# Sample steps spread over the stages, deeper rings for sample data, and row factors of two norms applied later

## The reference, cut to what matters

```
def decoder_layer(x, mk, mv, s0, buf, pos0, p):
    mix, s_new, buf_new = token_mix(rmsnorm(x, p['norm_mix_g']), s0, buf, pos0, p)
    h = x + mix
    h = h + cross_attn(rmsnorm(h, p['norm_x_g']), mk, mv, p['w_xq'], p['w_xo'])
    h = h + sq_relu_mlp(rmsnorm(h, p['norm_mlp_g']), p['w_up'], p['w_down'])
    return h, s_new, buf_new
# token_mix: proj = xn @ w_in -> q, k, v, gz, og, u, ga, gb
#   log_a = log_sigmoid(gz @ w_gk_up + b_gk) / 16
#   o, s_new = gla(q, k, v, log_a, s0): S_t = diag(a_t) S_{t-1} + k_t^T v_t, o_t = q_t S_t
#   branch_a = (rmsnorm(o, gla_norm_g) * silu(og)) @ w_branch_a
#   branch_b = pool_mix(u) @ w_branch_b       (trailing means of 2, 4, 8, 16 rows)
#   mix = (sigmoid(ga) * branch_a + sigmoid(gb) * branch_b) @ w_out
# cross_attn: softmax(q k^T / 16) v, 4 heads, 256 memory rows;  sq_relu_mlp: relu(x @ w_up)**2 @ w_down
```

## Time and profile before

| | |
|---|---|
| median of three runs | 1592.8 us (1590.46 to 1640.49) |
| profiled execution | 1591.72 us |
| its span on the slowest core | 1590.2 us (other cores from 1567.2) |
| PE, DVE, ACT, POOL busy | 84%, 40%, 29%, 13% of the span |
| mean granted TensorE clock of that core | 0.938 of full speed |
| moved by DMA | 265.59 MB, mean 167 GB/s |

### The profile page before, as it was taken

How to read it: one execution, slowest core, us unless ns; L and a number is a source line. 1 busy time by engine, 2 the same in 40 slices (tenths; PEclk the granted TensorE clock), 3 DMA queues, 4 the chain that set the end, 5 groups by cost and what they waited for, 6 DMA issues and landing times.

```text
span 1590.2 us, 21667 instructions; the slowest of 8 cores (1567.2 to 1590.2 us)
## 1 busy us (share of the span) xinstructions
PE 1343.2 (84%) x7848; PEld 659.4 (41%) x7848; DVE 641.9 (40%) x1105; ACT 462.3 (29%) x931; POOL 206.8 (13%) x284
## 2 busy tenths in 40 slices
PE   0884988999999989974879999999987449999997
PEld 0341533444445434432334544544443225444443
DVE  1352322544545325542355623553425014345334
ACT  2252321531256215300104621531114115152111
POOL 3122010310102002100010200300111112020000
PEclk9997899999999999976889999999998759999998
DMA  9969799859896699789875522525688852420232
GB/s 205 176 126 196 150 216 182 202 110 179 221 227 164 153 211 264 163 232 256 196 233 201 190 80 106 146 93 199 165 188 202 191 141 95 159 107 27 107 121 99
DMA packets 49252, 265.59 MB, mean 167 GB/s; under 512 B 6294, under 2 KB 6750, under 8 KB 25452
## 3 DMA queue, kind: packets, MB, share of 16 engines
q0 software_dynamic: 18336, 93.77, 36.4%
q1 hardware_dynamic: 30812, 170.43, 30.1%
HBM read 302.31 MB, written 56.36 MB: 226 GB/s over the span
## 4 chain that ended last, share of the span: by engine, by line
PE 63%; DMA 27%; DVE 3%; issue 3%; ACT 2%; POOL 1%; SPq 1%; DVEq 0%; POOLq 0%; ACTq 0%
PE pb L738 57%; DMA wt_45<-wu 5%; PE pb L750 3%; DMA kv_131<-cv 2%; DMA pmf<-wpmT 2%; PE pb L771 2%; DMA sgs<-s0f_85 2%; DMA mv<-tmp_89 2%; DMA wt_45<-wscratch 2%; DMA s0f_84<-sgla 2%; DMA kv_131<-ckT 1%; DMA wt_43<-wu 1%; DMA wscratch<-wt_45 1%; PE pb L761 1%; DMA s0b_116<-sgla 1%
## 5 line engine op out<-in xcount | busy, mean ns | idle before, releaser
L807 DVE TENSOR_TENSOR xh<-pb,xh 128x512 f32<-128x512 f32 x160 | 110.4, 691 | 131.1 <-PE pb L738 130.7
L807 POOL TENSOR_TENSOR stat<-stat,ncols 128x1 f32<-128x1 f32 (+2 forms) x87 | 59.0, 684 | 554.8 <-DVE stat L813 554.8
L795 ACT ACTIVATE tmp_86<-pb 128x512 f32<-128x512 f32 (+2 forms) x66 | 38.8, 587 | 246.6 <-PE pb L738 220.1
L738 PE MATMUL pb<-actT,wt_46 128*128 128x512 bf16 (+2 forms) x472 | 100.8, 368 | 2.2 <-DVE actT L807 2.2
L738 PE MATMUL pb<-actT,wt_45 128*128 128x512 bf16 (+2 forms) x408 | 88.2, 366 | 3.5 <-DVE actT L807 2.8
L795 ACT ACTIVATE tmp_88<-pb 128x512 f32<-128x512 f32 (+2 forms) x67 | 39.4, 587 | 167.1 <-PE pb L738 125.0
L738 PE MATMUL pb<-actT,wt_44 128*128 128x512 bf16 (+2 forms) x376 | 81.4, 369 | 7.6 <-DMA wt_44<-wu 4.2
L738 PE MATMUL pb<-actT,wt_43 128*128 128x512 bf16 x320 | 71.7, 379 | 0.0
L738 PE MATMUL pb<-actT,wt_47 128*128 128x512 bf16 (+2 forms) x312 | 65.5, 363 | 2.2 <-DVE actT L807 1.5
L738 PEld LDWEIGHTS pb<-actT,wt_46 128*128 128x128 bf16 x472 | 44.7, 98 | 53.8 <-issue 4.0
L738 PE MATMUL pb<-wt_43,actT 128*128 128x512 bf16 x224 | 54.8, 397 | 9.2 <-DMA wt_43<-wscratch 7.0
(11 more groups left out here) (466 smaller groups left out, 2335.5 us busy)
## 6 DMA issues: line engine op xcount, KB each, us to landing
wt_46<-wscratch SPq DMA_DIRECT2D x18, 1024.0 KB
wt_45<-wscratch SPq DMA_DIRECT2D x17, 1024.0 KB
wt_44<-wscratch SPq DMA_DIRECT2D x16, 1024.0 KB
wt_47<-wscratch SPq DMA_DIRECT2D x16, 1024.0 KB
wt_43<-wscratch SPq DMA_DIRECT2D x15, 1024.0 KB
wt_43<-wu POOLq DMA_DIRECT2D x14, 1024.0 KB, 15.6
wt_44<-wu POOLq DMA_DIRECT2D x14, 1024.0 KB, 15.5
wt_45<-wu POOLq DMA_DIRECT2D x14, 1024.0 KB, 15.2
```

What stands on the lines that cost most here:

```text
L738: ins = e.matmul(out, l, r, start=(start and i == 0), stop=(stop and i == m - 1))
L795: return self.g.op("act", lambda e: e.activation(out=out, in_=in_, func=func, scale=scale, **kw), reads=rd, writes=wr, cost=c, tab=tab)
L807: return self.g.op(eng, lambda e: e.tensor_tensor(out=out, in0=in0, in1=in1, op=op), reads=[in0, in1], writes=[out], cost=self.vcost(eng, ...
```

## The change

It has six parts.

1. DMAs get `ahead`: a DMA may not be issued before PE has reached the matmul that lies so many microseconds of recorded PE cost in front of its place in the program (60 for units, 30 for all else). The scheduler's prices of DMAs and of small POOL operations change too.
2. Units: all of the first tile's units are cast, and the up units alone are stored then; all others are cast again in tile 1 and stored there.
3. Start: the first rows are loaded first, v0 stands ahead of the forget gate in tile 0, and `precompute` begins after k, with one step per chunk.
4. States: no casting load; ACT copies `s0f` into `s0b`. The ring of `s0f` has four buffers in the back up to down(1), two in down(2) and down(3), and four more in xh's rows in the next tile's front. Steps: after each up unit but the first, after every second row block of a down, and at eight places of the next front; what is left is drained in tile 2 before gb0.
5. Keys have five buffers and values six (four in xh's rows). Value steps lie at v1, k, q, the chunks, u1 and the four branch units of tile 3, and are drained before the output projection.
6. Norms 2 and 3: ACT copies each half row of xh to xn unscaled, so that the transpose needs no row factor. Norm 2's factor is the scale of the softmax's exponent and multiplies the row maximum. Norm 3's, squared, scales the product of down as it is added, since relu(r y)^2 = r^2 relu(y)^2. One of the two products with the softmax sums goes from POOL to DVE.

```
 def op(self, eng, fn, ..., tab=None, ahead=None):
+        if eng == "pe":
+            self.peclk += cost
+            self.pelog.append((self.peclk, i))
...
+        if ahead is not None:
+            k = bisect.bisect_right(self.pelog, (self.peclk - ahead, 1 << 60)) - 1
+            if k >= 0:
+                deps[self.pelog[k][1]] = 0
...
-                s = max(t + c + 1.2, dma_free)
-                dma_free = s + o.nb
-                o.end = dma_free + 0.8
+                s = max(t + c + 1.4, dma_free)
+                dma_free = s + o.nb * 1.08
+                o.end = dma_free + 1.8
...
-        self.s0f = [g.sb(f"s0f{i}", Q + 16384 + 4096 * i, [128, 4, 256], F32) for i in range(2)]
+        self.s0m = [g.sb(f"s0f{i}", o, [128, 4, 256], F32) for i, o in enumerate((Q + 16384, Q + 20480, UR, UR + 6144))]
+        self.s0a = [g.sb(f"s0g{i}", XH + 4096 * i, [128, 4, 256], F32) for i in range(4)]
...
+        self.kvm = kv + [g.sb(f"km{i}", o, [128, 2048], BF16) for i, o in enumerate((Q + 16384, Q + 20480, UR + 4096))]
+        self.kva = kv + [g.sb(f"va{i}", XH + 4096 * i, [128, 2048], BF16) for i in range(4)]
...
-        elif times == 0 and name[:2] != "bp":
-            cast, store = True, idx % 3 == 0
-        elif times == 1 and idx % 3 != 0 and name[:2] != "bp":
-            cast, store = True, True
+        elif name[:2] == "bp":
+            cast, store = False, False
+        elif times == 0 or (times == 1 and name[:2] != "up"):
+            cast, store = True, times == 1 or name[:2] == "up"
...
-            self.dma("pool", flat, src, nb=5.6)
+            self.dma("pool", flat, src, nb=5.0, ahead=60.0)
...
             self.hook(nm, u)
+            if first and nm == "k":
+                self.gen["pre"] = self.precompute()
+                self.step("pre")
...
+            self.step("V")
+            self.step("G")
             if first:
-                self.step("pre", 2)
+                self.step("pre")
...
         def O_(s):
...
+            xns[s] = self.ring("xn", self.xn)
             for n in range(2):
...
                 self.stt("dve", xs, self.pb[bs[n]][:, :], 0.5, xs, ALU.mult, ALU.add)
-            xns[s] = self.norm_rows(self.xh[:, s, :])
+                self.cp("act", xns[s][:, n * 512:(n + 1) * 512], xs)
+            rs2[s] = meansq(s)
+            self.rstd(rs2[s], 128)
+
+        def meansq(s, st=None):
+            st = self.st4() if st is None else st
+            self.act(self.ring("ogs", self.ogs)[:, :], self.xh[:, s, :], AF.Square, scale=1.0 / 32, accum=st[:, 0:1])
+            return st
...
+                self.ts("dve", nm[:, 2 * hp:2 * hp + 2], nm[:, 2 * hp:2 * hp + 2], rs2[s][:, 0:1], ALU.mult)
...
-                    self.act(t[:, h * 256:(h + 1) * 256], self.pb[b][:, h * 256:(h + 1) * 256], AF.Exp, bias=nm[:, j:j + 1],
-                             accum=sm[:, j:j + 1])
+                    self.act(t[:, h * 256:(h + 1) * 256], self.pb[b][:, h * 256:(h + 1) * 256], AF.Exp, scale=rs2[s][:, 0:1],
+                             bias=nm[:, j:j + 1], accum=sm[:, j:j + 1])
...
-                self.tt("pool", Pn[:, 2 * hp:2 * hp + 2, :], pf[hp][:, :].rearrange("p (h m) -> p h m", m=256),
+                self.tt("dve" if hp else "pool", Pn[:, 2 * hp:2 * hp + 2, :], pf[hp][:, :].rearrange("p (h m) -> p h m", m=256),
...
-            xns[s] = self.norm_rows(self.xh[:, s, :])
+                self.cp("act", xns[s][:, n * 512:(n + 1) * 512], xs)
+            rs3[s] = meansq(s, self.r3[:, s, :])
+            self.ts("dve", rs3[s][:, 0:1], rs3[s][:, 0:1], EPS, ALU.add)
+            self.recip(rs3[s][:, 0:1], rs3[s][:, 0:1])
...
-                    self.tt("dve", xs, self.pb[b][:, :], xs, ALU.add)
+                    self.stt("dve", xs, self.pb[b][:, :], rs3[s][:, 0:1], xs, ALU.mult, ALU.add)
                 if each is not None:
                     each(s)
-                self.step("G")
+                if s % 2 == 0:
+                    self.step("G")
...
-            self.dma("pool", sb_[:, :, :].rearrange("p h v -> p (h v)"), I["sgla"][i], nb=1.4)
+            self.cp("act", sb_[:, :, :], sf[:, :, :])
...
-            kv = self.ring("kv", self.kv)
+            kv = self.ring("kvm", self.kvm)
...
-            kv = self.ring("kv", self.kv)
+            kv = self.ring("kva", self.kva)
```

More of the change, by code:

```diff
@@ L1 @@
+import bisect
 import contextlib
@@ L638, in alloc @@
         self.eBs = small("eBs", [128, 4, 16], F32)
+        self.r3 = small("r3", [128, 4, 4], F32)
         self.stat = small("stat", [128, 24, 4], F32)
@@ L841, in scan, with dma @@
                          reads=[d0, d1], writes=[out], cost=0.13 + 0.0021 * self.nfree(out))
-    def dma(self, q, out, in_, nb=None, rtok=(), wtok=()):
+    def dma(self, q, out, in_, nb=None, rtok=(), wtok=(), ahead=30.0):
         if nb is None:
@@ L900, in program @@
         I = self.I
-        self.consts()
         self.gen = {}
-        self.pend = None
+        self.dma("sp", self.cols[:], I["cols"][:, :])
         for s in range(4):
             self.dma("sp", self.land[s][:, :], I["xp"][s * 128:(s + 1) * 128, :])
-        for s in range(4):
-            self.norm_in(s)
+        self.consts()
         for s in range(4):
@@ L999, in vgroup @@
             self.cp("act" if n == 0 else "dve", self.vt[:, s, n * 512:(n + 1) * 512], self.pb[b][:, :])
-            self.step("V")
-        vgroup(u, 0, 0)
+            if n:
+                self.step("V")
+            if s % 2:
+                self.step("G")
+        if not first:
+            gzp()
+        self.hook("gz")
+        u = self.W("v0")
+        vgroup(u, 0, 0)
+        if first:
+            for s in range(1, 4):
+                vgroup(u, 0, s)
+            gzp()
+            u = self.W("v1")
+            vgroup(u, 1, 0)
         for h in range(4):
@@ L1012, in tile @@
             self.act(cur[:, h, :], Bc[:, :].rearrange("p (c t) -> p c t", t=128)[:, :, 127], AF.Exp, scale=-1.0 / 16)
-        for s in range(1, 4):
-            vgroup(u, 0, s)
-        self.hook("v", 0, u)
-        u = self.W("v1")
-        for s in range(4):
+        if not first:
+            for s in range(1, 4):
+                vgroup(u, 0, s)
+            self.hook("v", 0, u)
+            u = self.W("v1")
+        for s in range(1 if first else 0, 4):
             vgroup(u, 1, s)
@@ L1133, in tile @@
             self.consts4()
+        if ti == 2:
+            self.drain("G")
         for n in range(2):
@@ L1165, in tile @@
             self.drain("pre")
+        self.drain("V")
         for s in range(4):
@@ L1260, in up @@
                 self.hook("up", 2 * c + j, u)
-                self.step("G")
+                if c + j:
+                    self.step("G")
                 self.step("K")
@@ L1303, in tile @@
             self.drain("P")
+        self.s0set = "u"
         down(2, nxt)
         down(3, last)
-        self.drain("G")
         self.drain("K")
```

47 lines of the change are left out of this document (25 added, 22 removed).

## The result

The changed kernel takes 1476.2 us (median), 0.926 of the time before (95% interval 0.924 to 0.929): faster by 117 us where the prediction had 148. The profiled execution took 1476.3 us, on a slowest core other than before's.

The account below looks back on a forecast made before the run. Three stretches where PE waits (tile 0's front, tile 1's back, tile 3's front) set the end; the rest is PE-bound. Terms -30 + 13 - 59 + 6 - 74 - 4 = -148 from 1591.7 gave 1444 us, range 1400 to 1475.

Parts of the forecast that it names:

- Tile 0's front: Tile 0 up to the output projection: 225 us of transfers at a share of 0.94 give 239 us, -30.
- the early start: Start of tile 0: PE begins at about 24 us, not 52, which alone gives little since DMA sets the stage.
- Tile 1's front: Tile 1 up to the output projection: units cast again and stored, 156 us of transfers, 166 us, +13.
- Tile 1's back: Tile 1's MLP stage: casting loads gone, four state buffers, 15 us left for SP's queue: 145 us, -59.
- the ring: Tile 1's back: four state buffers instead of two halve the cycle of a state step from 12.8 to 6.4 us.
- the first rival: DMA throughput alone holds tile 1: its back 178 us, tile 0's front 247, 1485 us in all; chance 0.16.
- Tile 2's front and back: Tile 2: front +6 for the last state steps, back 128 to 135 us as key steps end there.
- Tile 3's front: Tile 3 up to the output projection: tile 2's 141 us plus 6 for value matmuls, 147 from 228, -81.
- The fourth rival: Tile 3's front: the spread does nothing for values, half of -81 stays lost, 1484 us; chance 0.05.
- Norms: Middles of all four tiles: norms 2 and 3 without row factors before the transpose win -4 us together.
- The in-order queues: Second rival: waits move from PE and SP to ACT's state copies and POOL's value loads, 1503 us; chance 0.08.
- the third: Rival for tiles 2 and 3: late unit loads cost 7 us each, 1682 us with half late; chance 0.02.

Follow-up runs that it names:

- old rule for units: Changed kernel with the former rule: in tile 0 every third unit is stored, in tile 1 the others are cast and stored; ratio 0.9324.
- late start: Changed kernel with the first four row factors held until the third weight unit lands, pmT ahead of them on POOL; ratio 0.9408.

## Why the prediction was right, and where its sum was off

The forecast was 1444, the measurement 1476.2. By stages, from its own terms to the windows above, the 32 us are: tile 3's front +15, the fronts of tiles 1 and 2 and tile 1's back +5, +4 and +5, tile 0's front -3, the four middles +1 together, backs and tail +1, and +4 for a gain of the norms that did not come. The prices that the experiments put on the parts (values 7 and 37, states 17, start 23, units 10, norms 1, bound 5) come to 100 of the 117 us, if they add, which the two halves of the states do not.

**Tile 0's front, forecast 239, measured 236.** The size was right and half of the reason wrong. The prediction had 225 us of bytes at a share of 0.94 set the stage and the early start give little; the stage holds 0.92 x 236 = 217. The old rule for units puts 13 us back, which agrees with the bytes of its stores (14.7), though a store also keeps its slot until it has landed. But the late start alone puts 18 us back with no byte added. A start 38 us later costs half of that, so the 27 us between 49 (wgz before) and 22 are worth some 13 us if that proportion holds: an estimate. The step that failed took the DMA engines as busy whatever PE does; with five slots they stop when PE does not free one.

**Tile 1's front, 166, measured 171.** Casts with stores lengthen it, as the term said, and more than by bytes alone. That the size came out is partly luck: the stage holds 0.86 x 171 = 147 us of transfers, where the term had 156, and stands at a share of 0.86, where it had 0.94. (Its lower bound of 153 us could not hold its own 156 us of transfers.) PE waits 6.3, 5.1 and 4.8 us there for units and for ACT. The neighbouring core, below, did it in 156.

**Tile 1's back, 145, measured 150; SP's waits for states forecast under 60, measured 72, against 119 before** (36.6 and 25.8 of the earlier trace rows with 36.3 and 20.6 for the other buffer). Right in size, not in reason. The argument gave the gain to the ring, with the bytes as the first rival. The runs say neither alone: undoing either one costs 23 us, undoing both 17, so the step that took the ring to halve a step's cycle by itself failed. Part of the rest goes with the rule for units, by which six up units are loaded in place of cast: the old rule costs 22 us over this back, the middle ahead and the front behind it in its profiled execution, 10 in the ratio of the whole. What the new places of the state steps give is open. By the first rival the ring gives nothing; without it the back takes 167 us, with it 150, so it does count once the casting loads are gone.

**Tile 2's front and back, 147 and 135, measured 151 and 134.** As forecast within 4 us.

**Tile 3's front, 147, measured 162: the largest miss.** The term took tile 2's old front of 141 us and added 6 for the value matmuls. What it removed was right: the ring's waits of the earlier trace rows are down to 3.3 us. Two steps failed. First, the front's own work: PE is busy 150 us there at a clock of 0.99, 14 more than in tile 2's old front, so 147 could not be reached. The 256 value matmuls take 8.6 us of that, not 6 (9.0 already in the trace before), and 4.4 us are keys: their last matmuls start at 1127.8 us, 15 us into this front, where the prediction ended them in tile 2. Second, ten value loads cost 6 us even when nearly no wait is for a value buffer; without them PE's waits there are all under 1 us. The fourth rival, that the spread does nothing for values, is refuted: the places alone are worth 37 us.

**Norms, -4 forecast.** Not found: +1 for undoing, within 6 us either way. The step that failed took the middle's idle PE time (1.5 us) as a wait for the row factor. In the trace before, PE's waits for normed rows in the four middles are 0.4, 0.4, 0.2 and 0.7 us, 1.7 together, and in the changed kernel it waits 2.3, 0.8 and 2.8 us in tiles 0, 2 and 3 for the product left on POOL. The price of ACT was too low besides: copies at 587 ns, and the exponentials as they were; they cost 90 ns more each, 64 in a kernel, 5.8 us of ACT. That ACT was on the path is not shown. The Trainium skill, ScalarE: Activation LUTs, section "What ACT_TABLE_LOAD costs", adds about 93 ns for each operand that is a column of a tile; the two rows, 563 and 473, agree.

**The other rivals.** The in-order queues: ACT waits 37 us for state loads in tile 1's back (14.8 and 22.1 for two buffers), but PE waits only 8.2 us for such a copy. The late unit loads of the third: none in tiles 2 and 3 above 1 us.

**The signs it named.** Four came out otherwise than the forecast had them: v0's first matmul at 29.6 us, not 24; SP's waits for state buffers of 72 us, not under 60; tile 3's front of 162 us with a value wait of 3.3, not under 155 and 2; and tile 2's middle at 58 us (55 before), where PE waits 2.1 us for an ACT copy.

## What to carry to other kernels

Where a stage is long because sample steps stand close together, try to spread them first; for the values the places were worth 37 us and the ring 7. Undo each half of a double change by itself and then both: here either half alone looked worth 23 us and both together 17. A stage in which the DMA share is full is not bound by the DMA engines alone when their buffers are freed by another engine: move the other one's start and see. And look at a share in short windows before adding transfers to a stage: a mean of 0.57 held 27 us at 0.99.

## What the runs showed that was not expected

The eight cores do the same work, but not in the same time: they go in pairs of which one is behind. The cores' spans and granted clocks in the changed kernel's profiled execution:

```profile
core 4: 1444.4 us, clock 0.977
core 5: 1472.5 us, clock 0.965
core 6: 1474.5 us, clock 0.969
core 7: 1441.7 us, clock 0.978
```

Of cores 0 and 1 it is 1466.0 and 1439.8, of 2 and 3 1445.8 and 1474.3: in each pair one is 26 to 33 us behind, and which one changes between executions. The windows of core 7 by the same seams, tile 0's front and tile 1's front:

```profile
0.00:225.00 225.00, 178.95 (x967) 88.09 (x968) 82.30 (x143) 75.57 (x148) 44.15 (x67) 0.96 0.95 184
387.00:543.00 156.00, 147.43 (x853) 71.73 (x853) 64.51 (x111) 62.67 (x128) 19.73 (x25) 0.99 0.91 222
```

It is 11 and 15 us ahead of core 6 in these two and 10 in tile 1's back, where transfers count, and level within 2 us in the backs of tiles 0, 2 and 3. So tile 1's front is 156 or 171 us, by which core of a pair one reads, and the kernel's time is that of the one behind. The Trainium skill, HBM Reference, section "Specifications (TRN2)", says that the two cores of a pair share the bandwidth of one memory. The rows agree in part: the three stages that differ by 10 us and more stand at a DMA share of 0.83 to 0.92 on core 6. But tile 0's back (0.88) and tile 3's front (0.80) are level, and in tile 2's front (0.46) core 7 takes 5 us longer. No run here shows where the two meet, or why one of them loses.

Small stores were the other surprise: 16 stores of 8 KB held SP 5.8 and 11.7 us, 0.36 and 0.73 us each, and ACT stood 13.8 us until they had landed.
